# A two-block model kernel: two feature pairs by halves at the joints, the residual's place lent to expert weights

## The reference, cut to what matters

```
x = x + mixer_layer(rmsnorm(x, norm_mix))
h = rmsnorm(x, norm_ffn)
x = x + hier_moe(h)              # 32 experts, 1024 -> 2*256 -> 1024, weights per token
h = layer_norm(rmsnorm(x, norm_final), ln_in_g, ln_in_b)
for l in range(2):
    a = concat(diff_attention(q, k, v), fourier_mix(u) @ w_f + b_f)   # q, k, v, u = h @ w_in
    h = layer_norm(ALPHA * h + a @ w_o, ln1_g, ln1_b)
    f = silu(h @ w_gate) * (h @ w_up)                                 # 2816 features
    h = layer_norm(ALPHA * h + f @ w_down, ln2_g, ln2_b)
```

## Time and profile before

| | |
|---|---|
| runs, median (lowest, highest) | 2003.53 us (2000.45, 2007.01) |
| the profiled execution, its own time | 2006.64 us |
| its span in the trace | 2005.4 us |
| busy: PE, PEld, DVE, ACT, POOL | 1838.4, 1449.7, 958.5, 777.3, 394.9 us |
| moved by DMA | 264.43 MB |
| expert stage | about 490 to 742 us |
| final stage, mixer 0, wo 0, ffn 0 | about 742, 798, 960, 1032 us on |
| mixer 1, wo 1, ffn 1 | about 1407, 1570, 1639 us on |

### The profile page before, as it was taken

One profiled execution on the slowest core, in us unless ns is written; L12 is line 12 of the kernel. 1 busy time (PEld: TensorE's weight loads), 2 busy tenths in 40 slices (PEclk: granted clock), 3 DMA queues, 4 the chain that ended last, 5 costly groups with the idle time before them and its releaser, 6 DMA issues.

```text
span 2005.4 us, 26563 instructions
## 1 busy us (share of the span) xinstructions
PE 1838.4 (92%) x10396; PEld 1449.7 (72%) x10396; DVE 958.5 (48%) x1881; ACT 777.3 (39%) x1436; POOL 394.9 (20%) x438
## 2 busy tenths in 40 slices
PE   7999999996998754998999999999999999999997
PEld 6888777785544424776778888787876778888786
DVE  4458776663311015968454433234868454333234
ACT  3344476221433234665253233115566252332212
POOL 1019155102222111243011111000233012111001
PEclk9999999996999996998999999999998999999999
DMA  4244200576999983211323333232211233333231
GB/s 162 80 113 126 95 2 2 168 286 242 381 383 401 394 308 125 74 53 43 105 85 100 100 95 95 89 100 70 77 64 43 84 95 98 101 95 95 87 103 53
DMA packets 134884, 264.43 MB, mean 132 GB/s; under 512 B 11616, under 2 KB 92128, under 8 KB 122464
## 3 DMA queue, kind: packets, MB, share of 16 engines
q1 hardware_dynamic: 116320, 228.35, 33.1%
q10 hardware_dynamic: 13312, 25.90, 3.8%
q0 software_dynamic: 5120, 8.40, 1.3%
HBM read 254.22 MB, written 16.78 MB: 135 GB/s over the span
## 4 chain that ended last, share of the span: by engine, by line
PE 54%; DMA 9%; DVE 7%; ACT 3%; issue 2%; POOL 1%; PEld 1%; PEldq 0%; ACTq 0%; POOLq 0%; SPq 0%; DVEq 0%
PE b L507 15%; PE b L508 15%; PE b L509 15%; DMA m<-in_w_gate_up 6%; PE b L2023 3%; ACT m L622 2%; DVE m L2736 1%; DMA m<-in_w_down 1%; PE b L2561 1%; PE b L2048 1%; PE b L2543 1%; PE b L2529 1%; DMA s_h<-m 1%; ACT m L690 1%; DVE m L694 1%
## 5 line engine op out<-in xcount | busy, mean ns | idle before, releaser
L507 PE MATMUL b<-m,m 128*128 128x512 f32 (+3 forms) x2060 | 782.0, 380 | 28.4 <-DVE m L636 8.8
L508 PE MATMUL b<-m,m 128*128 128x512 f32 (+3 forms) x2060 | 772.6, 375 | 0.0
L509 PE MATMUL b<-m,m 128*128 128x512 f32 (+3 forms) x2060 | 772.5, 375 | 0.0
L493 DVE TENSOR_TENSOR m<-m,m 128x1024 fp32r<-128x1024 f32 (+1 forms) x212 | 278.2, 1319 | 497.5 <-ACT m L483 496.6
L507 PEld LDWEIGHTS b<-m,m 128*128 128x128 f32 x2060 | 392.6, 191 | 105.8 <-issue 22.1
L509 PEld LDWEIGHTS b<-m,m 128*128 128x128 f32 x2060 | 392.4, 190 | 67.5
L508 PEld LDWEIGHTS b<-m,m 128*128 128x128 f32 x2060 | 393.1, 191 | 64.1
L483 ACT ACTIVATE m<-m 128x1024 fp32r<-128x1024 f32 (+1 forms) x236 | 245.7, 1048 | 484.2 <-PE b L509 458.0
L2986 POOL TENSOR_TENSOR m<-m,m 128x512 fp32r<-128x512 f32 x44 | 71.1, 1636 | 422.1 <-ACT m L2932 422.1
L2023 PE MATMUL b<-m,m 128*64 128x256 f32 x1024 | 126.7, 390 | 27.5 <-DMA m<-in_w_gate_up 26.2
L2023 PEld LDWEIGHTS b<-m,m 128*64 128x64 f32 x1024 | 73.6, 139 | 78.9 <-issue 38.6
(11 more groups left out here) (339 smaller groups left out, 1896.2 us busy)
## 6 DMA issues: line engine op xcount, KB each, us to landing
m<-in_w_gate_up SPq DMA_DIRECT2D x64, 1024.0 KB
m<-in_w_gu SPq DMA_DIRECT2D x88, 512.0 KB, 3.5
m<-in_w_down SPq DMA_DIRECT2D x32, 1024.0 KB
m<-in_w_in SPq DMA_DIRECT2D x48, 512.0 KB, 3.8
m<-in_w_down SPq DMA_DIRECT2D x44, 512.0 KB, 3.7
m<-in_w_in SPq DMA_DIRECT2D x20, 448.0 KB, 3.6
m<-in_w_o SPq DMA_DIRECT2D x16, 512.0 KB, 3.8
s_gt<-m ACTq DMA_DIRECT2D x16, 256.0 KB, 2.1
```

Of the source, the lines that this page charges most:

```text
L493: e.tensor_tensor(flat(wlo[HX[i]], i), flat(raw[RX[i][0]], i), fr(flat(whi[HX[i]], i)), ALU.subtract).then_inc(sem("w_lo"), 1)
L507: e.matmul(out, xh, yh, start=start, stop=False, skip_group_check=True)
L508: e.matmul(out, xh, yl, start=False, stop=False, skip_group_check=True)
L509: return e.matmul(out, xl, yh, start=False, stop=stop, skip_group_check=True)
```

## The change

- `PAIRS` gets two more places, the four tiles of X1. SP stores X1 to DRAM (`sync_keep`) when the output product has been added, and loads it back (`sync_state`) once the last pair in its place is used. DVE's first sum waits for that (`state`).
- SP's order is: loads before the ring, `sync_keep`, three ring pairs, the store of H2's last tile (until now ACT's), the other pairs, four `mix0` chunks, `sync_state`, the three gain loads (`sync_gains`, until now ACT's), then all eight Y2 loads.
- `mix0`'s first chunk gets the fourth place too; its four chunks are split at the start of the final stage. In `scalar_final` the last `scaled` comes behind `gained_act` of tile 2.
- `feat_halves` takes two pairs: first half of both, then second half of both, and counts `w_used` for each chunk. The K pair leaves `tensor_mixer`, the first up pair leaves `tensor_ffn`. At the barrier joints turn 3 comes behind the second feature tile instead of the first, and the layer norms split two more chunks at tile 3.
- In the mixer the constants come ahead of the Q and K parts, and chunks 4 and 5 are split between them.
- Layer 1 uses the banks with the two halves exchanged (`lb`, `swapped`); layer 0's down product starts on banks 4 to 7.
- `free_down` waits for the banks of step 9 and the first two low parts; `after_down` waits for two more with each chunk.

```
-TAIL, GATED, RING, MERGED, GAINS = 4, 10, 16, 22, 30
-PAIRS = [(4, 5), (6, 7), (8, 9), (30, 31), (10, 11), (12, 13), (14, 15), (0, 1), (2, 3), (16, 17), (18, 19), (20, 21), (22, 23), (24, 25), (26, 27), (28, 29)]
+TAIL, GATED, RING, MERGED, GAINS, STATE = 4, 10, 16, 22, 30, 32
+PAIRS = [(4, 5), (6, 7), (8, 9), (30, 31), (10, 11), (12, 13), (14, 15), (0, 1), (2, 3), (16, 17), (18, 19), (20, 21), (22, 23), (24, 25), (26, 27), (28, 29), (32, 33), (34, 35)]
...
+        X1D = nc.dram_tensor("s_x1", [S, D], F32).ap()
         Y2 = nc.dram_tensor("s_y2", [2 * S, D], F32).ap()
         chunks, CH, twins = weight_chunks(io)
         WHOLE = range(CH["up0"], CH["mix0"])
         LOADS, RX, landed = raw_places(len(chunks), CH["up0"], CH["mix0"])
-        HX, HB = halves_places(len(chunks), (CH["gu0"], CH["mix1"], CH["gu1"]), WHOLE)
+        HX, HB = halves_places(len(chunks), (CH["mix0"], CH["gu0"], CH["mix1"], CH["gu1"]), WHOLE)
...
+        for cell, load, reload in ((STATE, "x2", "ya2"), (STATE + 2, "x3", "ya3")):
+            goes_on[f"w_raw{cell}"] = (load, 16)
+            goes_on[reload] = (load, 16 + 16 * landed[cell])
...
+        raw2 += [X1[:, 2 * i:2 * i + 2, :] for i in range(2)]
...
+                elif cells[0] >= STATE:
+                    e.wait_ge(*at("kept", 64))
+                    e.wait_ge(*at("n2_x", 8))
+                    e.wait_ge(*at("rms_sq", 12))
...
-        def feat_halves(e, name, c0, xhi, xlo, bs, u, amid):
-            w = [chunk(e, c0), chunk(e, c0 + 1)]
+        def feat_halves(e, names, c0, xhi, xlo, bs, u, amid, free):
+            w = []
             for half in range(2):
                 c = slice(256 * half, 256 * half + 256)
                 e.wait_ge(*at("tr_lo", 8 * u + 4 * half + 4))
-                for f, k in [(f, k) for f in range(2) for k in range(8)] if half == 0 else [(f, k) for k in range(8) for f in range(2)]:
-                    hi, lo = w[k // 4]
-                    sl = slice(f * P, f * P + P)
-                    m = mm3(e, bank[bs[f]][:, c], hi[:, k % 4, sl], lo[:, k % 4, sl], xhi[:, k, c], xlo[:, k, c], k == 0, k == 7)
-                    if half == 1 and k == 7 and f == 0:
-                        m.then_inc(sem("mm_" + name), 1)
-                    if half == 0 and k == 7:
-                        amid(f)
-            m.then_inc(sem("w_used"), 2)
+                for q in range(2):
+                    if half == 0 and q == 1:
+                        free(e)
+                    for f, k in [(f, k) for f in range(2) for k in range(8)] if half == 0 else [(f, k) for k in range(8) for f in range(2)]:
+                        if half == 0 and f == 0 and k % 4 == 0:
+                            w.append(chunk(e, c0 + 2 * q + k // 4))
+                        hi, lo = w[2 * q + k // 4]
+                        sl = slice(f * P, f * P + P)
+                        m = mm3(e, bank[bs[2 * q + f]][:, c], hi[:, k % 4, sl], lo[:, k % 4, sl], xhi[:, k, c], xlo[:, k, c], k == 0, k == 7)
+                        if half == 1 and k == 7 and f == 0:
+                            m.then_inc(sem("mm_" + names[q]), 1)
+                        if half == 0 and k == 7:
+                            amid(2 * q + f)
+                        if half == 1 and k % 4 == 3 and f == 1:
+                            m.then_inc(sem("w_used"), 1)
...
+                if t == 3:
+                    lo_to(e, chunk_to + 2)
...
         def scalar_layer_norm(e, n, hi, banks, chunk_to):
             for t in range(NT):
+                if t == 3:
+                    hi_to(e, chunk_to + 2)
...
+            return (lambda t: one(t - 1) if t > 0 else None), (lambda n: one(3) if n == 1 else None)
...
-            store_normed(e, 3)
...
-            hi_to(e, CH["mix0"] + HL)
-            e.dma_start(gF, io["norm_final"].partition_broadcast(P)).then_inc(sem("gF"), 16)
-            e.dma_start(gL, io["ln_in_g_2"].partition_broadcast(P)).then_inc(sem("gL"), 16)
-            e.dma_start(bL, io["ln_in_b_2"].partition_broadcast(P)).then_inc(sem("gL"), 16)
...
+        def sync_gains(e):
+            last = max(i for i, cells, _ in LOADS if cells[0] in (TAIL + 4, GAINS))
+            e.wait_ge(*at("w_used", last + 2))
+            e.dma_start(gF, io["norm_final"].partition_broadcast(P)).then_inc(sem("gF"), 16)
+            e.dma_start(gL, io["ln_in_g_2"].partition_broadcast(P)).then_inc(sem("gL"), 16)
+            e.dma_start(bL, io["ln_in_b_2"].partition_broadcast(P)).then_inc(sem("gL"), 16)
+        def sync_keep(e):
+            for t in range(NT):
+                e.wait_ge(*at("mg_x1", 4 + t + 1))
+                e.dma_start(X1D[t * P:t * P + P, :], X1[:, t, :]).then_inc(sem("kept"), 16)
+        def sync_state(e):
+            e.wait_ge(*at("w_used", max(i for i, cells, _ in LOADS if cells[0] >= STATE) + 2))
+            for t in range(NT):
+                e.dma_start(X1[:, t, :], X1D[t * P:t * P + P, :]).then_inc(sem("state"), 16)
         def sync_final(e):
             e.wait_ge(*at("over", 1))
             added_up(e)
             for t in range(NT):
+                e.dma_start(YA[2 * t], Y2[t * P:t * P + P, :]).then_inc(sem(f"ya{2 * t}"), 16)
...
-            feat_halves(e, "fh0", CH["mix0"], NHhi, NHlo, (4, 5), 2, lambda f: turn(3) if f == 0 else None)
+            feat_halves(e, ("fh0", "k0"), CH["mix0"], NHhi, NHlo, (4, 5, 6, 7), 2, lambda n: turn(3) if n == 0 else None, no_wait)
         def scalar_final(e):
             e.drain().then_inc(sem("over"), 1)
-            added_up(e)
-            for t in range(NT):
-                e.dma_start(YA[2 * t], Y2[t * P:t * P + P, :]).then_inc(sem(f"ya{2 * t}"), 16)
             e.dma_start(LNT, io["c_lnT"]).then_inc(sem("lnT"), 16)
+            hi_to(e, CH["mix0"] + 4)
             for i in range(6):
                 if i < 4:
                     e.wait_ge(*at("f_sum", i + 1))
                     e.wait_ge(*at("rms_sq", SQUARES[2] + i))
                     e.activation(scr3, X1[:, i, :], ACT.Square, scale=math.sqrt(1e-5 / D), accum_out=st3[:, 8 + i:9 + i]).then_inc(sem("rms_sq"), 1)
-                if 0 <= i - 1 < 4:
-                    t = i - 1
+                def scaled(t):
                     e.wait_ge(*at("ln_nm", t + 1))
                     e.activation(X1[:, t, :], YA[2 * t + 1], ACT.Identity, bias=ln_n[:, t:t + 1], scale=ln_r[:, t:t + 1]).then_inc(sem("ln_ap"), 1)
+                if 0 <= i - 1 < 3:
+                    scaled(i - 1)
+                if i == 2:
+                    e.wait_ge(*at("lnT", 16))
                 if 0 <= i - 2 < 4:
-                    if i == 2:
-                        e.wait_ge(*at("lnT", 16))
                     gained_act(e, 0, i - 2, NHhi, B03)
-            hi_to(e, CH["mix0"] + 1 + HL)
+                if i == 4:
+                    scaled(3)
...
+            lo_to(e, CH["mix0"] + 4)
...
+                    if i == 0:
+                        e.wait_ge(*at("state", 64))
...
+        def lb(l):
+            return bank[4 * l:] + bank[:4 * l]
+        def swapped(l, banks):
+            return tuple(b ^ (4 * l) for b in banks)
...
-            gemm_feat(e, f"k{l}", c0 + 2, NHhi, NHlo, 8, (6, 7), no_wait)
...
-            for x in range(2):
-                q0_done(e, l, x)
-                e.activation(QT[0][:, x, :], bank[4 + x][:, :], ACT.Copy, scale=qsc[:, x:x + 1]).then_inc(sem("qk0_h"), 1)
-            hi_to(e, c0 + 3 + HL)
             e.wait_ge(*at("c1", 16 * (l + 1)))
             e.activation(C1s[0], c1, ACT.Copy).then_inc(sem("spl_h"), 1)
             e.wait_ge(*at("wf", 16 * (l + 1)))
             e.activation(wfR[0], wf, ACT.Copy).then_inc(sem("spl_h"), 1)
             e.wait_ge(*at("lam", 2 * l + 1))
             e.activation(lamb[:, 2:4], lamb[:, 0:2], ACT.Exp).then_inc(sem("lam_x"), 1)
+            for x in range(2):
+                q0_done(e, l, x)
+                e.activation(QT[0][:, x, :], lb(l)[4 + x][:, :], ACT.Copy, scale=qsc[:, x:x + 1]).then_inc(sem("qk0_h"), 1)
+            hi_to(e, c0 + 5)
             for x in range(2, 4):
                 q0_done(e, l, x)
-                e.activation(KT[0][:, x - 2, :], bank[4 + x][:, :], ACT.Copy).then_inc(sem("qk0_h"), 1)
+                e.activation(KT[0][:, x - 2, :], lb(l)[4 + x][:, :], ACT.Copy).then_inc(sem("qk0_h"), 1)
+            hi_to(e, c0 + 6)
...
-            behind, amid = turns(e, 1 + 2 * l, B47)
-            gemm_tail(e, f"wo{l}", [(c0 + n, (WO_K[n - 4], WO_K[n - 4] + 1)) for n in (5, 6, 7)], CThi, CTlo, B03, behind)
-            feat_halves(e, f"fg{l}", CH[f"gu{l}"], NHhi, NHlo, (0, 1), 3 + 2 * l, amid)
+            behind, amid = turns(e, 1 + 2 * l, swapped(l, B47))
+            gemm_tail(e, f"wo{l}", [(c0 + n, (WO_K[n - 4], WO_K[n - 4] + 1)) for n in (5, 6, 7)], CThi, CTlo, swapped(l, B03), behind)
+            feat_halves(e, (f"fg{l}", f"up{l}"), CH[f"gu{l}"], NHhi, NHlo, swapped(l, (0, 1, 2, 3)), 3 + 2 * l, amid, lambda e: e.wait_ge(*at(f"res_wo{l}", 8)))
...
-                o, c0 = 4 * (i % 2), CH[f"gu{l}"] + 4 * i
```

(30 more changed lines are left out.)

72 lines of the change are left out of this document (33 added, 39 removed), and 4 rows, old and new, of the table goes_on.

## The result

The changed kernel takes 2015.88 us (median of 11 runs, 2009.78 to 2017.69) where the kernel before takes 2005.29 on the same chip (11 runs, 2000.45 to 2008.30): a ratio of 1.005, with a 95% interval of 1.0042 to 1.0059. It is slower by some 10 us; the forecast was +2.2. The profiled execution took 2016.24 us, its span is 2014.9.

What follows compares the result with a forecast made beforehand. Weights (DMA) were taken to bound the expert stage, PE and its few waits the second block. Terms -5.5 + 0.5 + 9.5 + 8.0 - 10.3 = +2.2 us gave 2008.8 profiled, 2005.7 against the median; range 1995 to 2014.

Steps and rivals of the forecast that it cites:

- Experts: Expert stage and way into the second block: prefetching two more pairs brings the first Y2 sum to 750.6, -5.5 us.
- rival B: End of expert stage gives nothing, as reload, gains and Y2 share one queue: +7.7 us, 2011.2; chance 0.17.
- The loss shrinks to about 1 us: Start of experts: transfer lost at 484 to 500 us falls from 9.1 to about 1 us, weights ending 6.5 us earlier.
- 22.1 us: End of experts: w_in, residual, gains, first Y2 pair and landing, counted behind the weights' end, up to the first Y2 sum.
- I take 5.5: First gather of the experts: its length amid full queues, taken between its 3.86 us and the store's 14.27.
- First joint: Final stage to mixer 0, no barrier: PE saves 1.48 us, but step 0 waits for DVE, at 812.7; +0.5 us.
- Two wo joints: wo to ffn, both layers: barrier uncovered, gate 1 3.0 us later, 1.7 us of clock lost; +4.75 us each.
- Mixer 1: Joint from ffn to mixer 1: exposed loads and copies put step 0 13.4 us behind the barrier; +8.0 us.
- free_down: Down product, both layers: PE's 3.43 us wait for POOL and 1.7 us of clock loss go; -10.3 us in all.
- D's nine us of DMA: Rival, faster: DMA gives 9 us at the experts and the wo joints' clock doesn't drop; -4.7 us, 1998.8; chance 0.18.
- E's free barriers: Rival at the barrier joints: next work is ready, so barriers cost nothing; sum -23.1 us, 1980.4; chance 0.09.
- C's extra clock loss: Rival: clock costs 1.7 us more at each wo joint, mixer 1 starts 2 us later; +7.6, 2011.1; chance 0.13.

Runs made afterwards that it cites:

- gather_ahead: Two runs: changed kernel with several mends, SP's last five or two expert weight pairs held until the first gather landed; 1984.75 and 1982.23 us, against 1979.82 without holding.
- pool_waits: Changed kernel plus one wait: in each mixer's first four steps GpSimd's low part comes only behind VectorE's gain and offset; 2006.30 us, ratio 1.000 to the kernel before.
- forced_holds: Kernel before, one wait exchanged: in each mixer's first four steps GpSimd's low part is released just ahead of VectorE's gain and offset; 2018.68 us, ratio 1.0071.
- split_ahead: Changed kernel with the next two chunks' high and low parts made ahead of the barrier at all three barrier joints; 1997.79 us, ratio 0.9958 to the kernel before.

## Why the prediction was wrong

**The number.** The forecast was 2.2 us over the kernel before, and it is 9.5 between the profiled executions; 2015.88 lies 1.9 us above the range. Two things make it: 4.6 us at the Y2 sum, and 7.8 us of holds in the mixers; the other terms together came out 5 us better than forecast.

**Experts (-5.5, measured -0.9).** Wrong. It is nearly rival B, which was to decide "when the first Y2 sum starts at 756 or later"; it starts at 755.14, later than the 754 at which "the expert stage was misjudged". The step that failed is "The loss shrinks to about 1 us": 3.7 us of transfer were still lost up to 500 us. The first place came free at 495.5 us and not at 492, and with the DMA engines at a share of 1.01 only 310 GB/s were moved at 488 to 492 us; why it was not 390 stays open. So the weights ended 3.1 us earlier instead of 6.5. The sum behind them, "22.1 us" and 1 us allowed, took 23.4, which is right by luck: the residual's loads did not follow at full rate but waited for their place, the scatter got faster (6.57 us to Y2's issue instead of 8.53), and Y2's own first pair slower. By the rule on rings quoted for B (the Trainium skill, "DMA: Bandwidth & Descriptors", section "Queues, rings and completion order") both gather and scatter wait longer. The gather did, the scatter didn't. For the gather "I take 5.5" was wrong as well: 8.09. "Experts then start 2 us earlier": 1.6 later in this pair of executions. The two gather_ahead runs fit what the prediction said of that start, that in a stage bound by DMA a start some us earlier is no gain.

**First joint (+0.5, measured +0.4).** Right.

**The mixers' steps (0, measured +3.8 and +4.0).** The missing term, and the larger failure. The prediction says of mixer 1 "DVE has no pause in the first steps, so nothing gives it back", and took the lengths of those steps as fixed. They are fixed only as long as GpSimd's low part doesn't meet the gain or the offset. The timeline of the kernel before had a case, 3.32 us for L643 at 834.08, beside 1.22 in the other steps; the prediction does not mention it. pool_waits takes the holds away, forced_holds adds them, and the time follows both ways.

**Two wo joints (+4.75 each, measured +4.2 and +4.1).** Right in mechanism and size: 2.54 us at gate 1 (forecast 3.0) and 1.7 for the clock (forecast 1.7) in layer 0. That both come from the uncovered splits is shown by split_ahead, where both are gone. The split of 48 products into 96 cost what the rows said: the 256-column products of the changed kernel start 0.12 us apart, as in the earlier trace rows.

**Mixer 1 (+8.0, measured +6.4).** Right in mechanism; step 0 came 12.4 us behind the barrier instead of 13.4, and the loads' landing was about 3 us of that. A further 2.0 us were given back: 1.2 between steps 13 and 14 of mixer 1, and 0.9 from there to the turn in wo of layer 1. In that last stretch TensorE waits 1.97 us for L493 at 1583.96 in the kernel before and 1.98 for the same at 1596.31 in the changed one; the granted clock was 0.83 at 1580 to 1590 us before (1.7 us lost) and 1.00 at 1590 to 1610 after. Why the clock fell behind the one and not behind the other, and what gave the rest, stays open; it was no part of the forecast, and luck.

**free_down (-10.3, measured -5.2 and -5.4, 10.6 in all).** Right, and alone it makes the kernel 0.6% faster.

**The rivals.** B came true, D's nine us of DMA and E's free barriers did not; C's extra clock loss didn't come. What decided beside B, the holds, was no rival at all.

## What to carry to other kernels

When work is moved ahead of a barrier, ask what hid the things behind it, and move those too: here two chunk splits ahead of the barrier turned each wo joint from 4.2 us of loss into 2.9 of gain, but moved nothing at mixer 1, where the waits were others. Before a stage's lengths are taken as fixed, compare the longest and the shortest execution of each line in it: a VectorE operation that is now and then 2 us longer is meeting GpSimd, and which of them comes first can change with a shift of 1 us that has nothing to do with either. A load that waits for its place is issued late, whatever the queue's order, so what stands behind it should be only what is needed next. And where a stage ends differs from execution to execution, here by 4.6 us in the kernels without the expert part, so a term of 1 or 2 us needs more than one pair of traces.
